# Attention outputs and probabilities turned by VectorE blocks and DRAM instead of TensorE, output norm one frame later

## The reference, cut to what matters

```python
q, k = partial_rope(rms_norm(q)), partial_rope(rms_norm(k))      # two parts of 64
p = softmax(mask(q @ k.T))                                        # per part
a = p[0] - lam * p[1]
o = rms_norm(a @ v, subln_g) * (1 - lambda_init)
mixed = concat(o_fox, o_diff); x = x + mixed @ w_out
```

## Time and profile before

| | |
|---|---|
| median of the runs | 1046.23 us |
| profiled execution | 1046.72 us |
| its span, first to last instruction | 1044.9 us |
| PE, weight loads, DVE, ACT, POOL busy | 99%, 90%, 71%, 75%, 2% |
| granted TensorE clock | 1.00 of full speed |
| DMA | 217.77 MB, 208 GB/s in the mean |

### The profile page before, as it was taken

How to read it: one execution, slowest core, us unless ns; L and a number is a source line. 1 busy time by engine, 2 the same in 40 slices (tenths; PEclk the granted TensorE clock), 3 DMA queues, 4 the chain that set the end, 5 groups by cost and what they waited for, 6 DMA issues and landing times.

```text
span 1044.9 us, 16398 instructions
## 1 busy us (share of the span) xinstructions
PE 1038.9 (99%) x5327; PEld 940.0 (90%) x5327; DVE 744.6 (71%) x1237; ACT 785.3 (75%) x1376; POOL 20.9 (2%) x27
## 2 busy tenths in 40 slices
PE   9999999999999999999999999999999999999998
PEld 8999999999988888888888888888889988888887
DVE  7788878778767566577776776876867678766664
ACT  7787666788858884879788788798797778755553
POOL 0101010000000000000000000000000000000000
PEclk9999999999999999999999999999999999999999
DMA  9756676676766666666566565665655766666664
GB/s 352 235 168 191 192 229 205 212 242 229 240 212 197 204 199 204 203 214 201 189 218 197 192 223 189 201 220 183 220 182 193 232 204 202 203 202 206 205 203 145
DMA packets 75580, 217.77 MB, mean 208 GB/s; under 512 B 15864, under 2 KB 18688, under 8 KB 75392
## 3 DMA queue, kind: packets, MB, share of 16 engines
q1 hardware_dynamic: 75376, 216.79, 63.5%
q10 hardware_dynamic: 144, 0.20, 0.1%
HBM read 212.69 MB, written 4.27 MB: 208 GB/s over the span
## 4 chain that ended last, share of the span: by engine, by line
PE 95%; DMA 2%; DVE 1%; ACT 1%; SPq 0%; issue 0%; DVEq 0%; ACTq 0%
PE ps L621 14%; PE ps L620 14%; PE ps L622 14%; PE ps L651 7%; PE ps L649 7%; PE ps L650 7%; PE ps L397 7%; PE ps L399 7%; PE ps L398 7%; PE ps L598 3%; PE ps L596 3%; PE ps L597 3%; DMA raw<-in_win 2%; PE ps L419 1%; PE ps L410 0%; DMA p_read<-p_scratch 0%
## 5 line engine op out<-in xcount | busy, mean ns | idle before, releaser
L1138 DVE TENSOR_TENSOR w_lo<-raw,w_hi 128x1024 fp32r<-128x1024 f32 (+1 forms) x406 | 463.5, 1147 | 245.7 <-ACT w_hi L697 242.3
L697 ACT ACTIVATE w_hi<-raw 128x1024 fp32r<-128x1024 f32 (+1 forms) x406 | 398.4, 988 | 166.9 <-PE ps L651 74.8
L622 PE MATMUL ps<-w_hi,xs 128*128 128x512 f32 (+1 forms) x704 | 263.6, 374 | 0.0
L620 PE MATMUL ps<-w_hi,xs 128*128 128x512 f32 (+1 forms) x704 | 263.6, 374 | 0.0
L621 PE MATMUL ps<-w_lo,xs 128*128 128x512 f32 (+1 forms) x704 | 263.6, 374 | 0.0
L397 PE MATMUL ps<-w_hi,xs 128*128 128x384 f32 (+1 forms) x496 | 165.8, 334 | 0.5 <-DVE w_lo L1138 0.5
L399 PE MATMUL ps<-w_hi,xs 128*128 128x384 f32 (+1 forms) x496 | 161.9, 326 | 0.0
L398 PE MATMUL ps<-w_lo,xs 128*128 128x384 f32 (+1 forms) x496 | 161.9, 326 | 0.0
L620 PEld LDWEIGHTS ps<-w_hi,xs 128*128 128x128 f32 x704 | 133.2, 189 | 17.1
L621 PEld LDWEIGHTS ps<-w_lo,xs 128*128 128x128 f32 x704 | 133.2, 189 | 17.1
L622 PEld LDWEIGHTS ps<-w_hi,xs 128*128 128x128 f32 x704 | 133.2, 189 | 17.1
(11 more groups left out here) (167 smaller groups left out, 938.8 us busy)
## 6 DMA issues: line engine op xcount, KB each, us to landing
raw<-in_wrest SPq DMA_DIRECT2D x278, 512.0 KB, 3.7
raw<-in_win SPq DMA_DIRECT2D x117, 384.0 KB, 3.8
raw<-in_wrest SPq DMA_DIRECT2D x16, 384.0 KB, 2.9
p_scratch<-pdT SPq DMA_DIRECT2D x11, 192.0 KB, 2.1
p_read<-p_scratch SPq DMA_DIRECT2D x44, 48.0 KB, 3.1
xtok<-in_xtok SPq DMA_DIRECT2D x4, 512.0 KB, 14.0
xv<-in_xtok SPq DMA_DIRECT2D x4, 512.0 KB, 5.9
raw_ahead<-in_w SPq DMA_DIRECT2D x5, 392.0 KB, 8.1
```

Source lines behind the costliest of these rows:

```text
L620: pe.matmul(o, xh, wh, start=(k == 0), stop=False, skip_group_check=True)
L622: last = pe.matmul(o, xl, wh, start=False, stop=(k == KT - 1), skip_group_check=True)
L697: act.activation(slot(w_hi, s, w), slot(raw, s, w), ACT.Copy).then_inc(hi_ready, 1)
L1138: dve.tensor_tensor(slot(w_lo, s, w), slot(raw, s, w), f32(slot(w_hi, s, w)), ALU.subtract).then_inc(split_done, 1)
```

## The change

Four things are changed together.

1. The probabilities of heads 2, 3 and 15 go the way of heads 4 to 14 (`P0` 2, `P_STOP` 16): block transpose on DVE, store, four reads. Head 2's copy applies the scale that its PSUM copy applied.
2. The normalised output of each diff head goes the same way: `turn_o` on DVE, `store_o` and `read_o` on SP through a new DRAM tile `o_scratch`, and `mix_hi` and `mix_lo` read it from `o_read`. The transposes on PE are gone. This happens a frame later: head f-2's norm in frame f, behind split 1, and its high and low parts behind split 6.
3. In the frames of diff heads the copy into `pT` moves from piece 0 to piece 1, values and their sums from piece 2 to piece 4, the statistics to piece 5 and the guess to piece 6. Fox head 16's values go into the bank of its transposes.
4. In the output projection the eighth and ninth pieces change places, so that piece 7 of the first block comes behind piece 0 of the second. Head 16's steps there and the addition of the first block move one piece down.

```diff
-P0, P_STOP = 4, HEADS - 1
+P0, P_STOP = 2, HEADS
-TRAIL_AT = dict(values=2, sums=2, norm=2, turn=4, hi=5, lo=6)
+TRAIL_AT = dict(copy=1, values=4, sums=4, stats=5, guess=6)
+NORM_AT = dict(norm=1, mix=6)
-OUT_AT = dict(turn=1, scores=2, probs=4, values=5)
+OUT_AT = dict(turn=2, scores=3, probs=5, values=6)
+LAST_BLOCK_VALUES = 4
+OUT_ORDER = [(0, b) for b in range(7)] + [(1, 0), (0, 7)] + [(1, b) for b in range(1, 8)] + ...
...
+            def store_o(f):
+                sp.wait_ge(o_turned, f)
+                if f > 1:
+                    sp.wait_ge(o_landed, 64 * (f - 1))
+                sp.dma_start(o_d, onT[:]).then_inc(o_stored, 16)
+            def read_o(f):
+                sp.wait_ge(o_stored, 16 * f)
+                if f > 1:
+                    sp.wait_ge(dmix_lo, f - 1)
+                for j in range(4):
+                    src = o_d[:, j * 64:(j + 1) * 64].rearrange("(i r) c -> r i c", i=4)
+                    sp.dma_start(o_read[32 * j:32 * (j + 1), :].rearrange("r (i c) -> r i c", i=4), src).then_inc(o_landed, 16)
...
+                    if 4 <= f <= H + 2 and b == 1:
+                        store_o(f - 2)
+                    if 4 <= f <= H + 2 and b == 3:
+                        read_o(f - 2)
...
-                if not first:
-                    pe.wait_ge(mixlo_done, f - 1)
+                if kind == "diff" and not first:
+                    pe.wait_ge(onorm_done, f - 1)
...
-            def out_transposes(f):
-                pe.wait_ge(onorm_done, f)
-                for m in range(M):
-                    last = pe.transpose(bank(B_O, S + m * P, P), on[:, m * P:(m + 1) * P], ident)
-                last.then_inc(oturn_done, 1)
...
+                act.wait_ge(o_landed, 64 * f)
+                act.activation(by_blocks(mxt, 0), landed_o(), ACT.Copy, scale=sg[:]).then_inc(dmix_hi, 1)
...
+            def turn_o(f):
+                dve.wait_ge(onorm_done, f)
+                if f > 1:
+                    dve.wait_ge(o_stored, 16 * (f - 1))
+                dve.transpose(onT[:].rearrange("p (j m t) -> p j m t", j=4, m=M),
+                              on[:].rearrange("p (m j t) -> p j m t", j=4, m=M)).then_inc(o_turned, 1)
...
+                    for m in range(M):
+                        last = dve.scalar_tensor_tensor(out=by_blocks(mxt, 1)[:, m], in0=landed_o()[:, m], scalar=sg[:],
+                                                        in1=by_blocks(f32(mxt), 0)[:, m], op0=ALU.mult, op1=ALU.subtract)
+                    last.then_inc(dmix_lo, 1)
```

More of the change, by code:

```diff
@@ L429, in prob_transposes, with values @@
                 last.then_inc(pt_done, 1)
-            def values(f, p, kind, first=False):
+            def values(f, p, kind, first=False, o=B_O):
                 if isinstance(f, int) and P0 <= f <= H:
@@ L484, in attention_steps @@
                 if b == at.get("values"):
-                    values(f, p, kind)
+                    values(f, p, kind, o=B_T)
             def projection(f, par, b):
@@ L599, in out_piece @@
                 last.then_inc(piece_used, 1)
-            for b in range(8):
-                out_piece(0, b)
-                if b == 0:
-                    prob_transposes(HEADS - 1, "fox")
-                if b == 1:
-                    values(HEADS - 1, 0, "fox")
-                attention_steps(HEADS, 1, "fox", b, OUT_AT)
-            for blk in range(1, OUT_BLOCKS):
-                for b in range(8):
-                    out_piece(blk, b)
+            for g in range(8):
+                out_piece(g)
+                attention_steps(HEADS, 1, "fox", g, OUT_AT)
+                if g == LAST_BLOCK_VALUES:
+                    block_values(HEADS - 1, 0)
+            for g in range(8, OUT_PIECES):
+                out_piece(g)
             def up_piece(nb, k, banks, w):
@@ L805, in attention_steps @@
                 if b == at.get("values") and kind == "fox":
-                    mix_hi(f, kind)
+                    mix_hi(f, kind, B_T)
             def trailing_steps(f, b):
+                if b == TRAIL_AT["copy"]:
+                    copy_p(f - 1)
                 if b == TRAIL_AT["sums"]:
                     out_sums(f - 1)
-                if b == TRAIL_AT["norm"]:
+                if b == TRAIL_AT["guess"]:
                     out_guess(f - 1)
-                if b == TRAIL_AT["hi"]:
-                    mix_hi(f - 1, "diff")
             def forget_steps(b):
@@ L845, in frame @@
                         head_norm(f + 1, next_kind)
+                    if isinstance(f, int) and f == 4 and b == 1:
+                        mix_hi(1, "diff")
+                    if isinstance(f, int) and f <= H + 2 and b == NORM_AT["mix"]:
+                        mix_hi(f - 2, "diff")
                     if spill and b == 5:
@@ L1104, in up_batch @@
                         up_steps(nb - 1, s, 1 - par)
-                    if not post:
-                        x1_steps(OUT_BLOCKS - 1, s)
+                    if not post and s < 9:
+                        x1_steps(OUT_BLOCKS - 2 + (s > 0), (s + 7) % 8)
                     if not post and s == 13:
@@ L1323, in after_split @@
                     forget_bias(f)
-                if trail and b == TRAIL_AT["sums"]:
+                if trail and b == TRAIL_AT["stats"]:
                     out_stats(f - 1)
-                if trail and b == TRAIL_AT["norm"]:
-                    norm_o(f - 1)
                 if b == at.get("values") and kind == "fox":
-                    mix_lo(f, kind)
+                    mix_lo(f, kind, B_T)
             def parameters():
@@ L1403, in frame @@
                         turn_qk(f + 1, 1 - p)
+                    if isinstance(f, int) and f == 4 and b == 1:
+                        mix_lo(1, "diff")
+                    if isinstance(f, int) and f <= H + 2 and b == NORM_AT["norm"]:
+                        norm_o(f - 2)
+                        turn_o(f - 2)
+                    if isinstance(f, int) and f <= H + 2 and b == NORM_AT["mix"]:
+                        mix_lo(f - 2, "diff")
                     if spill and b == 5:
@@ L1734, in lay_out @@
     wo = np.concatenate([wo[H:], wo[:H]]).reshape(8, 2, P, OUT_BLOCKS, HALF, 2)
-    wo = wo.transpose(3, 0, 2, 1, 5, 4).reshape(-1, PW)
+    wo = wo.transpose(3, 0, 2, 1, 5, 4)
+    wo = np.concatenate([wo[blk, b] for blk, b in OUT_ORDER]).reshape(-1, PW)
     wu = np.asarray(w_up)[0].reshape(KT, P, 2, FT * P)
```

161 lines of the change are left out of this document (86 added, 75 removed).

## The result

The changed kernel takes 1051.41 us (median of 7 runs, 1049.43 to 1052.49), the kernel before 1046.46 us on the same chip (7 runs). That is 5.0 us more, where 1.1 more was forecast. The ratio is 1.0048, with a 95% interval of 1.0038 to 1.0057: slower, clear of what can be told from no change, and above the range that was predicted (1043.0 to 1050.4). The profiled execution of the changed kernel took 1052.32 us (span 1050.5), 5.6 us more than the one before.

The account below looks back on a forecast made before the run. PE was taken as the bound (95% of the chain). Terms -4.3 - 0.5 + 2.8 + 0.6 + 0.35 + 1.9 + 0.3 gave +1.1 us, 1047.3 us against a median of 1046.23; 8-in-10 range 1043.0 to 1050.4.

Parts of the forecast that it names:

- What comes off PE: PE loses output transposes (1.8 us), probability transposes of heads 2, 3, 15 (1.0) and waits before values (1.5): 4.3 us saved.
- the stall at 149 us: Frame 8's first piece: PE's wait of some 0.8 us behind the gates' scattered read shrinks by 0.5 us (0 to 0.8).
- (a): Frames 4 to 7, behind piece 2: transposes of q and k wait uncovered for POOL's rotate, 0.7 us each, 2.8 us.
- Rotate in time: Rival, faster: DVE's splits fall otherwise, the rotate ends 1.25 us sooner and its waits go; 1042.7 us, chance 0.17.
- lock rule: DVE and POOL share ports exclusively; without two-input DVE instructions beside it the rotate would end 0.65 + 0.6 us sooner.
- (b): End of piece 6, frames 5 to 7: ACT waits for the outputs' reads before the squares, 0.2 us each, 0.6 us.
- Reads late: Rival, slower: outputs' reads land late before ACT's squares, costing 0.8 us in each of frames 5 to 9; 1050.7 us, chance 0.2.
- (c): DVE's added work, the low-part pair in frame 10, delays a split PE needs in frame 11: 0.35 us (0 to 0.8).
- (d): Frame 8: the late chain behind the gates' read makes PE wait for the rotate, 1.9 us (1.4 to 2.6).
- (e): Frame 3: DVE turns head 2's probabilities ahead of the norms, so head 3's transposes wait 0.3 us (0 to 0.8).
- all bounds at their bad end: Case with every term at its worst bound: +5.8 us against the profiled execution of the kernel before.

Follow-up runs that it names:

- the second profile: The changed kernel run once more, with no edit: 1051.54 us (4 runs), ratio 1.0054 to the kernel before; its profiled execution took 1049.63 us.
- the last version: Changed kernel with values behind piece 2 (frames 5 to 9), norm after piece 5, outputs' parts in piece 7, gates' read in four: 1045.82 us, ratio 1.0003.

## Why the prediction was wrong

- **What comes off PE**: right. Eight pairs at 0.22, three groups at 0.33 (head 15's inside the out stage), the waits before values 1.5. But 0.9 of these waits and the stall at 149 us (0.5 in the forecast, 0.8 in the profile) differ between executions: I took one profile's accidents for terms. Nothing in the earlier trace rows says so; a second profile would.
- **(a) the rotate**: right, 0.69, 0.70, 0.70 and 0.69 us in frames 4 to 7. The later transposes took it away. The rival "Rotate in time" didn't come: the rotate's second half took 1.05 us in each of these frames. The lock rule of the Trainium skill ("SBUF — State Buffer", section "Who interferes with whom") gets one more row: in the last version's frame 5 DVE has only instructions of two columns beside the rotate's second half, and it took 0.46 us; in the changed kernel's frame 5 a split, which reads two tiles, lies beside it, and it took 1.05. The trace agrees.
- **(b) reads late**: this is the step that failed. I worked out when the reads land against the squares from one frame, took 0.2 us each for frames 5 to 7, and put frames 9 and 10 at nothing, without a reason. In frames 5 to 8 they cost next to nothing: in frames 5, 6 and 8 ScalarE waited for PE before the squares (0.3 us), in frame 7 for the reads (0.37 us), which made the group behind it 0.04 us longer. In frames 9 and 10 ScalarE's wait was 1.0 and 2.3 us, and PE lost 0.7 and 2.4. Counted from the squares of the frame before, the reads are issued after 12.6 to 12.8 us in frames 5, 6 and 8, after 13.4 in frame 9 and after 14.4 in frame 10 (14.6 in frame 7, behind the late load there, but those landed within 1.9 us). In frame 10 the 11 moves delay ScalarE's splits, and with them SP's load and the reads behind it. What delays them in frame 9 is open, but there PE is also earlier at the squares, since it has no rotate to wait for and half as many score matmuls. The rival "Reads late" had the mechanism with 0.20, from frame 5 on and by slow landings. Landings had a part in frame 10 alone (3.8 us at the longest, up to 3.1 in the others, 3.4 in the second profile); the rest was late issue and, in frame 9, the earlier PE. ScalarE in frames 7 and 8, and SP in frames 8 and 9:

```profile
149.59 0.51 ACT L821 ACTIVATE mixed<-o_read,sg 128x256 fp32r<-128x256 f32 x1 [0.37 <-DMA o_read<-o_scratch]
...
168.77 0.84 ACT L749 ACTIVATE sq<-ps,r 128x256 f32<-128x256 f32 x2 [0.31 <-PE ps L443]
```

```profile
162.94 1.80 SPq L351 DMA_DIRECT2D o_read<-o_scratch  x4
...
182.19 1.75 SPq L351 DMA_DIRECT2D o_read<-o_scratch  x4
```

- **(c) frame 11**: the place was right, the size and the cause weren't. 2.4 us and not 0.35, and 0.2 of it at most is DVE's pair of low parts, as the earlier reads show, which leave that pair where it is.
- **The clock**: not in the prediction at all. 1.7 us in six of eleven executions of the changed kernel; in its first profile the fall comes 1.4 us after the wait of 2.4.
- **Frame 4**: left out. I had the copy's place at piece 1 among what takes waits away, and didn't ask what stands behind it on ScalarE where the read is late: 1.2 us, shown by the copy at piece 2. Head 3's read of its probabilities is issued 4.9 us after its store (75.05 to 79.93), where in frame 9 it is 2.3.
- **(d) frame 8 and (e) frame 3**: too dark by 1.2 and 0.3 us. Frame 8 lost 0.74 like the others (1.15 in the second profile), frame 3 nothing.

Term by term as measured: -4.2 (off PE) - 0.8 (stall) + 2.8 (rotate, frames 4 to 7) + 0.7 (frame 8) + 0.7 + 2.4 (frames 10 and 11) + 1.2 (frame 4) + 1.7 (clock) + 1.1 (out stage without its group of transposes) = +5.6 us, where +1.1 was forecast. The out stage's 1.1 can't be told from what differs between executions, as the run with head 15 on PE says. That all bounds at their bad end gave +5.8 in the prediction, near to what was measured, is luck: they held 2.7 us for (b) in frames 5 to 7 and 2.6 for (d), where 0 and 0.7 came, and nothing for the clock, for frame 4 or for the reads of frames 9 and 10.

## What to carry to other kernels

An instruction that waits for a transfer is priced by what stands behind it on its engine, and in each frame apart: where one frame has more work on that engine, the transfer is issued later, and the same place in the order no longer covers it. Before a step is moved, list which steps share its buffer; here the values and the norm had to move together. And a wait seen in one profile of the kernel before is a term of the sum only if a second one shows it.

## What was not expected of the hardware

- After a wait of PE of 2.0 to 2.4 us the granted clock fell to half in some executions and not in others: six of eleven of the changed kernel, three of seven of the kernel before with the six copies, none of the twenty of the two versions with this wait gone. At this place it stays there for 3.4 us in every profile that shows the fall. Longer waits don't settle it: 2.7 us at the same place left it at 1.00 in the profile of the version with the copy at piece 2, and in the profile with the values back at piece 2, where PE waits about 3 us in each of six frames and before a projection matmul at 227 us, it fell once, in frame 5. What decides is open.
- The first dozen projection matmuls start 0.32 us apart in some profiles (from 5.4 to 8.9 us in the three together) and 0.16 in others: 1.5 us or so that belong to no edit. 0.32 us is the distance that projection matmuls have at half the clock at 213 us. The views print 1.00 for this stretch, but the trace has no entry for the clock there: its first one, of the full clock, begins at 8.9 us in that profile, where the distance changes to 0.16, and at 5.0 us in the first profile of the changed kernel. In five other profiles with a long slow start it begins within 0.3 us of the change too. So it looks like the lower level; no entry shows it.
